# Four transposes ahead of the first up step, and a weight split ahead of a scalar chain

## The reference, cut to what matters

```
mod = silu(c) @ ada_w + ada_b                      # 9 rows of 1024: sh1, sc1, g1, ... g3
u = x * (1 + sc1) + sh1
y = (silu(u @ ffn1_w_gate) * (u @ ffn1_w_up)) @ ffn1_w_down        # 1024 -> 2816 -> 1024
x = layer_norm(ALPHA * x + 0.5 * (1 + g1) * y, ln1_g, ln1_b)
...
log_a = (-8 * softplus(-rglru_lambda)) * r         # used much later, in the recurrence
```

## Time and profile before

| | us |
|---|---|
| median of 3 runs | 1932.71 |
| lowest and highest | 1931.93, 1935.97 |
| the profiled execution | 1933.65 |
| its span, first to last instruction | 1931.7 |
| TensorE busy in it | 1847.6 (96%) |
| VectorE, ScalarE, GpSimd busy | 1056.8, 818.1, 499.6 |

### The profile page before, as it was taken

How to read it: one execution, slowest core, us unless ns; L and a number is a source line. 1 busy time by engine, 2 the same in 40 slices (tenths; PEclk the granted TensorE clock), 3 DMA queues, 4 the chain that set the end, 5 groups by cost and what they waited for, 6 DMA issues and landing times.

```text
span 1931.7 us, 23120 instructions
## 1 busy us (share of the span) xinstructions
PE 1847.6 (96%) x8960; PEld 1509.1 (78%) x8960; DVE 1056.8 (55%) x1078; ACT 818.1 (42%) x864; POOL 499.6 (26%) x644
## 2 busy tenths in 40 slices
PE   4899999999999899999999999998999999999998
PEld 4778887887888587878788888877998867877877
DVE  6355555556887897455332323358652445645542
ACT  3222223237666766325533432255222547333351
POOL 0311111021899564002000000140104995201000
PEclk8999999999999899999999999999989999999999
DMA  8365555553333233433332223364733321552411
GB/s 311 131 195 174 174 171 180 156 179 132 109 109 118 78 131 110 151 132 104 103 98 97 88 87 90 92 188 169 153 88 122 116 93 43 170 160 99 142 44 44
DMA packets 204214, 247.84 MB, mean 128 GB/s; under 512 B 5899, under 2 KB 184875, under 8 KB 202091
## 3 DMA queue, kind: packets, MB, share of 16 engines
q1 hardware_dynamic: 185643, 171.27, 27.9%
q0 software_dynamic: 13472, 51.42, 9.1%
q10 hardware_dynamic: 5024, 24.12, 3.3%
HBM read 227.39 MB, written 19.40 MB: 128 GB/s over the span
## 4 chain that ended last, share of the span: by engine, by line
PE 70%; POOL 9%; DVE 8%; ACT 6%; issue 4%; DMA 2%; SPq 1%; DVEq 0%; ACTq 0%; POOLq 0%
PE ps L2091 21%; PE ps L2285 17%; PE ps L2157 11%; POOL conv_out L487 8%; PE ps L2121 3%; ACT w_hi L604 3%; PE ps L2426 2%; PE ps L2467 2%; PE ps L2622 2%; DVE w_lo L1224 2%; DVE ada_acc L1322 2%; PE ps L2540 1%; PE ps L2455 1%; DMA w_raw<-in_ffn_w_gate 1%; PE ps L2476 1%
## 5 line engine op out<-in xcount | busy, mean ns | idle before, releaser
L1224 DVE TENSOR_TENSOR w_lo<-w_raw,w_hi 128x2048 fp32r<-128x2048 f32 x158 | 370.2, 2343 | 552.1 <-ACT w_hi L604 549.8
L604 ACT ACTIVATE w_hi<-w_raw 128x2048 fp32r<-128x2048 f32 x156 | 298.4, 1913 | 662.1 <-PE ps L2285 238.2
L2091 PE MATMUL ps<-u_hi,w_hi 128*128 128x512 f32 x656 | 259.8, 396 | 6.8 <-DVE w_lo L1224 6.7
L2285 PE MATMUL ps<-u_hi,w_hi 128*128 128x512 f32 x656 | 258.3, 394 | 5.0 <-DVE w_lo L1224 5.0
L2285 PE MATMUL ps<-u_hi,w_lo 128*128 128x512 f32 x656 | 256.9, 392 | 0.0
L2285 PE MATMUL ps<-u_lo,w_hi 128*128 128x512 f32 x656 | 256.9, 392 | 0.0
L2091 PE MATMUL ps<-u_lo,w_hi 128*128 128x512 f32 x656 | 256.4, 391 | 0.0
L2091 PE MATMUL ps<-u_hi,w_lo 128*128 128x512 f32 x656 | 256.1, 390 | 0.0
L487 POOL TENSOR_TENSOR conv_out<-conv_out,conv_tap 128x512 f32<-128x512 f32 x120 | 195.2, 1627 | 80.6 <-ACT conv_tap L787 63.6
L2091 PEld LDWEIGHTS ps<-u_hi,w_hi 128*128 128x128 f32 x656 | 123.9, 189 | 35.5 <-issue 5.9
L2285 PEld LDWEIGHTS ps<-u_hi,w_hi 128*128 128x128 f32 x656 | 124.2, 189 | 30.9 <-issue 5.2
(11 more groups left out here) (505 smaller groups left out, 3311.3 us busy)
## 6 DMA issues: line engine op xcount, KB each, us to landing
w_raw<-in_w_in SPq DMA_DIRECT2D x44, 1024.0 KB, 5.1
ada_raw<-in_ada_w POOLq DMA_DIRECT2D x56, 512.0 KB, 5.1
w_raw<-in_ffn_w_gate SPq DMA_DIRECT2D x22, 1024.0 KB, 5.4
w_raw<-in_ffn_w_up SPq DMA_DIRECT2D x22, 1024.0 KB, 5.3
w_raw<-in_ffn_w_down SPq DMA_DIRECT2D x32, 704.0 KB, 4.6
ada_first<-in_ada_w SPq DMA_DIRECT2D x8, 1024.0 KB, 14.3
w_raw<-in_w_out SPq DMA_DIRECT2D x8, 1024.0 KB, 5.1
w_raw<-in_xa_wk SPq DMA_DIRECT2D x4, 1024.0 KB, 5.1
```

The lines of the kernel that those rows point to most:

```text
L604: A(WHI[:, slot], WRAW[:, slot], ACT.Copy).then_inc(s["w_hi"], 1)
L1224: V.tensor_tensor(WLO[:, slot], WRAW[:, slot], WHI[:, slot].bitcast(F32), ALU.subtract).then_inc(s["w_lo"], 1)
L2091: ins = M(PS[:, 2 * j + t, 0:n], w[:, j, at_:at_ + P], a[:, k, 0:n], start=(k == 0 and q == 0), stop=(k == KT - 1 and q == 2))
L2285: ins = M(PS[:, 2 * j + t], w[:, j, at_:at_ + P], a[:, k], start=(q == 0), stop=(q == 3 * KT - 1))
```

## The change

Two edits of order; nothing is computed differently. TensorE makes the four transposes of the parameter rows behind the first gate step, ahead of the first up step. VectorE makes the first split of `down1` (the chunk of the third half) behind the two first instructions of the decay chain; it stood behind the chain, the columns and the derived scales. The step is left out of `tiles` for the first iteration.

```
 def tiles(i):
     for j in range(4):
-        lo_step(ph, i, 4, j)
+        if not with_ada or not (isinstance(i, int) and i == j == 0):
+            lo_step(ph, i, 4, j)
...
 chain(V.tensor_tensor(LAM[:, 1], lam, LAM[:, 0], ALU.min))
+lo_step("down1", 0, 4, 0)
 step[0] += 1
...
 first_chunk()
+parameter_columns()
 chunk(0, 1)
-parameter_columns()
```

## The result

The changed kernel takes **1923.04 us** in the median of five runs (1922.19 to 1925.15); the kernel before, on the same chip, 1935.97 (1931.93 to 1939.54, five runs). The ratio is 0.9938, with a 95% interval of 0.9925 to 0.9950. So it is faster by 9.7 to 14.5 us of 1936. The direction and most of the size are as forecast, but the time lies 5.1 us above the predicted 1917.9 and 1.2 us beyond the range.

A forecast was written before the change was run, and what follows sets the result against it. The prediction took TensorE, 70% of the span, to bound the kernel, losing time where it waits or runs at its lower clock. Terms of -9.4 and -5.4 made -14.8, from 1932.7 to 1917.9 us; range 1913.8 to 1921.8.

The forecast's parts named there:

- Transposes free, wait of 5.0 gone: Second gate step: moved transposes add no TensorE time and its start moves from 69.46 to 64.4, -5.0 us.
- Cold matmuls, -2.9: Second gate step: without the wait its 48 matmuls run at the full clock, -2.9 us.
- First group, +1.1: First group of parameter columns: VectorE's round ends later than TensorE's step (0.5) and GpSimd's scaling slows sums (0.6), +1.1 us.
- Second group, -0.9: Second group of parameter columns: scaling ends earlier, so the 1.22 us wait shrinks to the steady 0.28, -0.9 us.
- Clock behind the second group, -1.65: From second to next parameter group: no clock fall any more, 23.20 us instead of 24.85, -1.65 us.
- Rival (a): The clock falls after the first parameter group, 1.65 us more, 1919.5 us; chance 0.17.
- Part one: First feed-forward block: the four transposes moved ahead of the first up step, -9.4 us in sum.
- Part two, -5.4: Down projection: split ahead of the decay chain removes a 3.0 us wait and 2.4 us of cold matmuls, -5.4 us.
- (e): Down projection: the removed wait only moves to the fourth half, up to 1923 us; chance 0.05.
- The rest shifts whole: Rest of the program: starts only from semaphores of this work, so the full -14.8 us reaches the end.
- The base: Whole kernel: the median of the kernel before, 1932.7 us, from which the gain was subtracted.
- (b): Elsewhere in the kernel: one or two clock falls more or fewer, 1914.6 to 1921.2 us; chance 0.19.

The follow-up runs named there:

- e5: The changed kernel with GpSimd's scaling of x_res cut to 8 of 512 columns of each tile: 1920.06 us, ratio 0.9918 to the kernel before.
- e11: The changed kernel unchanged, measured a third time in a later batch: 1922.22 us, ratio 0.9941 to the kernel before.
- e4: The kernel before once more, unchanged: 1935.26 us, ratio 0.9999 to the kernel before.
- e3: The kernel before with only the first down-projection split moved ahead of the decay chain: 1930.14 us, ratio 0.9974.
- e2: The kernel before with only the transposes moved ahead of the first up step: 1928.08 us, ratio 0.9963.

## Why the prediction was right in its places and wrong in its size

**Transposes free, wait of 5.0 gone: right.** 69.46 became 64.39, -5.07. **Cold matmuls, -2.9: right.** By the step's last matmul the shift is 75.04 - 82.98 = -7.94.

**First group, +1.1: right.** Its wait was 0.95, near the 0.86 that the prediction gave, and by the next up step it had cost 1.2 (shift -7.94 to -6.73); e5 shows which part is GpSimd's. One reading in it was wrong and did no harm: a group without a wait takes 0.81 us from its start to the next matmul (83.21 to 84.02 before), not 0.91; the group from 107.30 to 108.21 had waited.

**Second group, -0.9: right.** 1.22 became 0.29.

**Clock behind the second group, -1.65: the step that failed.** In the trace after, that fall is gone, but a fall behind the first group took its place: the stretch from the first to the second group is 24.86 us. Rival (a) named just this and got 0.17; by the six profiles it should have had about a third. That this shift is -13.0 after and -14.8 in e11, where the clock stayed, is this one outcome. And the fall that was credited as a sure gain was itself one execution's: e4, the same kernel, had 0.78 there and none, e3 had 1.11 and one. So the term should have been a difference of two chances, as far as so few profiles give them: -1.1 for a fall at the second group, seen in two of three profiles with the old order (1.65 x 2/3), and +0.55 for one at the first group, seen in two of six with the new one. Part one alone then makes -7.9 + 1.1 - 0.9 - 1.1 + 0.55 = -8.25, where e2 measured 7.2 with an interval of 4.5 to 9.9; the sum had -9.4.

**Part two, -5.4: right in its mechanism, its cold half 0.6 too large on average.** The wait and the cold half went, nothing became late behind them (next split at 319.82, no wait), and e3 measured 5.0. The chance against (e) was well placed. But the 2.4 for the cold matmuls was one execution's too: behind the same wait of 3.04 the twelve matmuls took 5.19 before, 4.27 in e4 and 4.46 in e2, against 2.86 at the full clock after. The mean price is 1.8, and part two -4.8.

**"The rest shifts whole": failed in part.** All work does start from semaphores, but not all from TensorE's. The prediction read rows 6 only as two waits of unlike outcome. It didn't ask why the wait at 1345.98 was only 1.80. It was short because TensorE was late there, with cold matmuls from 1312, while VectorE set the start. With the full clock at 1312 TensorE would have waited some 4 us there, as e2 did (4.09), and what it gains between the squares' sum and this point moves nothing. The prediction's own last sign of being wrong, a wait behind 400 us that grows, came true there (1.80 to 4.28). Of the 13.3 us that arrived, 2.6 were lost to a fall that the profile of before happened not to have. In other executions of before it is there (e4), so this moved the comparison of two profiles more than the comparison of medians.

**The base: failed, for 2.8 us.** Three runs gave 1932.71, 20 runs 1935.56, and single runs of the kernel lie from 1929.65 to 1939.54. On a base of 1935.56 the forecast sum would have given 1920.8, and a range as wide as the stated one 1916.7 to 1924.7, which holds the measured time. Of the miss of 5.1 us the base is 2.8 and the gain itself the rest, 2.3; by the ratios the gain was 11.4 to 12.0 where 14.8 was forecast. The terms as corrected above, -8.25 and -4.8, leave 13.05; from 1935.56 that is 1922.5, and the three medians of the changed kernel are 1923.04, 1924.45 and 1922.22. The range has a slip of its own: it was to be (b)'s bounds, 1914.6 and 1921.2, with the runs' spread of -0.8 and +3.3 around 1932.7 on top. Below that was added (1913.8); above it gives 1924.5, but the range ended at 1921.8.

**Open:** how many falls each kernel has on average was not counted; a profile shows one execution, and six or three of them bound a chance only roughly, so the corrected terms fit the measured gain but don't prove it. Nor was it tried what sets the time of the round trip before 1702: that wait was 3.30 before and from 2.72 to 4.81 in the others, 4.45 and 2.72 in two profiles of the same changed kernel, so it is no effect of an edit.

The Trainium skill, "SBUF — State Buffer", "Who interferes with whom", calls the port pair that VectorE and GpSimd share an exclusive lock, and says that a VectorE instruction with two inputs in SBUF contends with a GpSimd instruction that reads there. Contention there was, but no lock for the length of a GpSimd instruction (some 1.9 us here): four sums took 3.69 us against 3.11, with the scaling going on at the same time, and the measurement decides. The Trainium skill, "TensorE: Matmul & The Clock Gate", Part 1, says that the monitor runs freely; the two outcomes of 0.95 us in one kernel agree, and they are why a fall behind a short wait goes into the sum at its chance and into the range in full.

## What to carry to other kernels

A cold stretch seen behind a short wait in one profile is a chance, not a cost, and even behind a long wait its length is one execution's: credit it at its share of the profiles, and put its full price into the range on both sides. When a gain passes a later wait of the bounding engine, look at what the releasing engine did from its last common point: if its work has no gap, the start there moves only with that point, and an engine that looks barely late (1.80 us) may hide a wait of 4.3. Take the small vector work that nobody waits for out of the way of all the splits in a row, since moving one alone only hands the wait to the next; and put a small product that needs another engine's sums into the middle of a long step, where 0.5 us per round is saved here.

## What the runs showed of the hardware

- At the parameter groups TensorE's granted clock stayed at 2.4 GHz after each idle time of 0.28 to 0.30 us. After 0.95 to 0.97 it fell to 1.2 GHz in two profiles of six, after 0.78 not, after 1.11 and 1.22 it did. Behind 1.89 us near 829 it fell in six profiles of thirteen, behind 3.04 in three of three, after 3.92 to 5.01 each time in the rows shown. A fall behind a group cost some 1.65 us, one behind a wait of 4.1 to 4.4 us at the `u` start 2.5 to 2.8 in six profiles and 1.6 in a seventh (e3, wait 4.23).
- A fall can be free: at 1294 it came while TensorE was ahead of a wait, and made the wait shorter (1.70 for 2.96) with the start in the same place, 6.14 us behind the squares' sum.
- GpSimd's elementwise work on 128x512 beside them slowed four VectorE sums from 3.11 to 3.69 us, 0.15 us each.
- The wait that a row names is shorter than what it costs: a group behind a 0.28 us wait takes 0.50 us more of a round than one with none (23.22 against 22.72). The shown wait starts at the modelled end of the last matmul, 0.39 after its start, while its slot is 0.2266: 0.16 us that no row calls a wait. And a group that had waited takes 0.91 us to the next matmul, one that had not 0.81.
